# Delta-rule scan of a hybrid encoder layer: heads exchanged in four of the eight chunks, and the order of the work around them changed

## The reference, cut to what matters

```python
def step(state, inp):                     # per head: state is 64 x 64
    r_t, w_t, k_t, v_t, kk_t, a_t = inp
    s_kk = einsum('bhvk,bhk->bhv', state, kk_t)
    new = (state * w_t[:, :, None, :] - s_kk[..., None] * (kk_t * a_t)[:, :, None, :]
           + v_t[..., None] * k_t[:, :, None, :])
    read = state if reverse else new
    return new, einsum('bhvk,bhk->bhv', read, r_t)
```

## Time and profile before

| what | value |
|---|---|
| three runs | 1971.67, 1964.76 and 1939.02 us, median 1964.76 |
| the profiled execution | 1955.42 us, its span 1953.7 us |
| mean granted TensorE clock | 0.956 of full |
| PE busy, weight loads busy | 1723.0 us (88%), 1267.9 us (65%) |
| DVE, ACT, POOL busy | 1358.9 us (70%), 811.6 us (42%), 491.2 us (25%) |
| HBM traffic | 218 GB/s over the span |

### The profile page before, as it was taken

One profiled execution on the slowest core, in us unless ns is written; L12 is line 12 of the kernel. 1 busy time (PEld: TensorE's weight loads), 2 busy tenths in 40 slices (PEclk: granted clock), 3 DMA queues, 4 the chain that ended last, 5 costly groups with the idle time before them and its releaser, 6 DMA issues. The chain is left out here.

```text
span 1953.7 us, 42217 instructions
## 1 busy us (share of the span) xinstructions
PE 1723.0 (88%) x15366; PEld 1267.9 (65%) x15366; DVE 1358.9 (70%) x2513; ACT 811.6 (42%) x1327; POOL 491.2 (25%) x432
## 2 busy tenths in 40 slices
PE   3999999998688889888797699999888999999875
PEld 2787766876577778777645376666666667666532
DVE  4699996663567676765546578877766788888707
ACT  1222223441445455443300155655555566656501
POOL 2000000141644554451113013211111223332114
PEclk9899999999899999999997899999999999999988
DMA  8635853433323313222061389989888899999844
GB/s 274 193 99 173 271 171 99 130 113 98 79 44 63 66 44 72 44 61 60 3 242 54 143 314 339 371 337 345 304 304 301 314 347 345 343 351 346 326 200 199
DMA packets 259760, 389.97 MB, mean 200 GB/s; under 512 B 121923, under 2 KB 195841, under 8 KB 232240
## 3 DMA queue, kind: packets, MB, share of 16 engines
q1 hardware_dynamic: 239392, 354.28, 52.5%
q0 software_dynamic: 19872, 33.60, 4.9%
q10 hardware_dynamic: 367, 0.22, 0.1%
HBM read 368.33 MB, written 58.49 MB: 218 GB/s over the span
## 5 line engine op out<-in xcount | busy, mean ns | idle before, releaser
L2369 DVE TENSOR_TENSOR moe_w_lo<-moe_raw,moe_w_hi 128x1024 fp32r<-128x1024 f32 x272 | 315.1, 1220 | 42.8 <-ACT moe_w_hi L2295 42.6
L2295 ACT ACTIVATE moe_w_hi<-moe_raw 128x1024 fp32r<-128x1024 f32 x272 | 265.4, 1047 | 116.0 <-DMA moe_raw<-in_exp_up 115.6
L2249 PE MATMUL moe_pY<-moe_wd,moe_hT 128*128 128x512 f32 x544 | 248.1, 599 | 0.5 <-ACT moe_hT L2310 0.5
L2239 PE MATMUL moe_pH<-moe_w_hi,moe_x_hi 128*128 128x512 f32 x544 | 219.7, 404 | 12.0 <-issue 7.5
L2173 POOL DMA_INDIRECT moe_xg<-scratch_u2d,moe_idx x70 | 89.1, 1272 | 555.9 <-issue 240.4
L572 PE MATMUL proj_bank<-u_hi,w_hi 128*128 128x512 f32 x536 | 213.7, 399 | 8.4 <-PEq L74 6.8
L2239 PE MATMUL moe_pH<-moe_w_lo,moe_x_hi 128*128 128x512 f32 x544 | 214.3, 394 | 0.0
L2239 PE MATMUL moe_pH<-moe_w_hi,moe_x_lo 128*128 128x512 f32 x544 | 214.1, 394 | 0.0
L572 PE MATMUL proj_bank<-u_hi,w_lo 128*128 128x512 f32 x536 | 210.0, 392 | 0.0
L572 PE MATMUL proj_bank<-u_lo,w_hi 128*128 128x512 f32 x536 | 209.6, 391 | 0.0
L2249 PEld LDWEIGHTS moe_pY<-moe_wd,moe_hT 128*128 128x128 f32 x544 | 100.0, 194 | 100.3 <-issue 99.5
(11 more groups left out here) (414 smaller groups left out, 3139.9 us busy)
## 6 DMA issues: line engine op xcount, KB each, us to landing
moe_raw<-in_exp_gate SPq DMA_DIRECT2D x69, 1024.0 KB
moe_raw<-in_exp_up SPq DMA_DIRECT2D x69, 1024.0 KB
moe_wd<-in_exp_down SPq DMA_DIRECT2D x68, 1024.0 KB
w<-in_w_in SPq DMA_DIRECT2D x59, 512.0 KB, 7.0
pre<-in_ada_w SPq DMA_DIRECT2D x10, 2048.0 KB, 20.5
last_yb<-scratch_ybuf SPq DMA_DIRECT2D x4, 2560.0 KB, 25.5
scratch_rkv<-proj_st SPq DMA_DIRECT2D x24, 256.0 KB, 2.0
last_yb<-scratch_ybuf SPq DMA_DIRECT2D x4, 1536.0 KB, 19.8
```

What stands on the lines that cost most here:

```text
L2239: ins = nc.tensor.matmul(pH[:], a[:, k], w[p][:, k].rearrange("p w f -> p (w f)"), start=(k == 0 and n == 0), stop=(k == KC - 1 and n == 2))
L2249: ins = nc.tensor.matmul(pY[h][:], hT[:, f], wd[q][:, f, h * 512:(h + 1) * 512], start=(f == 0), stop=(f == 1))
L2295: nc.scalar.activation(w_hi[p][:, ks].rearrange("p k w f -> p w k f"), raw[p][:, :, ks], ACT.Copy) \
L2369: nc.vector.tensor_tensor(w_lo[p][:, ks].rearrange("p k w f -> p w k f"), raw[p][:, :, ks], w_hi[p][:, ks].rearrange("p k w f -> p w k f") ...
```

## The change

- **Exchanged heads.** In chunks 4 to 7 (c // NU is 1) what lies in time order has its heads exchanged: `to_time` writes head h to the other half's partitions, `to_channels` reads from the other half and writes back to the head's own. GB, GK and the four turns issue chunk u of the lower half and chunk u + 4 of the upper half alternately, into two banks; PR does it for banks 0 and 2, then 1 and 3. AC, MV, U, V and T4 stay with `by_head`, the inverse's blocks too.
- **Value products.** The output part of `base` becomes `values_read`. For the upper chunks all are issued after PR, for the lower ones with the state as before. Two semaphores come with it: `s_based` before a state's first product, `y_based` before the first lower chunk's output.
- **Order.** ZW, ZA are made for J+4 in place B5. GB moves from E (after PR) to a new place P (between AC and PR). TQ, TK, TB stand in one place each with both halves. ACT's `exps` stands ahead of C5.
- **DVE.** `scan(J + 3)` moves to the start of the job. The stages of `invert` stand as 0 between the reads of U4 and V4, 1 after those of V4, 2 between U5 and V5, 3 after V5 (before: 0 between U5 and V5, then 1 to 3 in a row). The reciprocals of the deviation and the first merge move to the end of the odd job and the start of the next. Three small instructions of stage 0 become subtractions of two tensors, with a tensor of zeros.

```diff
+FILL = {0: {"S0": (("TV", 0), ("TV", 1)), "C4": (("Z", 1), ("SS", 0)),
+            "B4": (("Z", 2), ("TQ", 0), ("TQ", 1)), "A4": (("Z", 3), ("TK", 0), ("TK", 1)), "C5": (("Z", 4), ("TB", 0), ("TB", 1)),
+            "B5": (("Z", 5), ("MV", 0), ("Z", 6), ("MV", 1), ("ZW", 0), ("ZA", 0), ("Z", 7), ("BO", 0), ("GK", 0), ("GK", 1),
                    ("MEAN", 0)),
+            "P": (("GB", 0), ("GB", 1))},
+        1: {"S0": (), "C4": (("Z", 1), ("VAR", 0)),
+            "B4": (("Z", 2), ("TQ", 0), ("TQ", 1)), "A4": (("Z", 3), ("TK", 0), ("TK", 1)), "C5": (("Z", 4), ("TB", 0), ("TB", 1)),
+            "B5": (("Z", 5), ("MV", 0), ("Z", 6), ("MV", 1), ("ZW", 0), ("ZA", 0), ("Z", 7), ("G", 0), ("GK", 0), ("GK", 1)),
+            "P": (("GB", 0), ("GB", 1))}}
...
-    of = {"Z": J - 1, "GB": J + 3, "GK": J + 1, "ZW": J + 3, "ZA": J + 3, "BO": p, "G": p, "SS": p + 2, "MEAN": p - 1,
+    of = {"Z": J - 1, "GB": J + 3, "GK": J + 1, "ZW": J + 4, "ZA": J + 4, "BO": p, "G": p, "SS": p + 2, "MEAN": p - 1,
...
-            self.take([("PR", J, k) for k in range(4)])
-            self.take(fills(J, "E"))
+            self.take(fills(J, "P"))
+            self.take([("PR", J, k) for k in (0, 2, 1, 3)])
...
+            def to_time(c, out, lhsT, rhs):
+                for h in range(2):
+                    ins = mm(out[HEADS[h ^ (c // NU)]], lhsT[HEADS[h]], rhs[HEADS[h]])
+                return ins
+
+            def to_channels(c, out, lhsT, rhs, start=True, stop=True):
+                for h in range(2):
+                    src = HEADS[h ^ (c // NU)]
+                    ins = mm(out[HEADS[h]], lhsT[src], rhs[src], start, stop)
+                return ins
...
+                o = [begin((name, q, X)) for X in range(2)]
                 for u in range(NU):
+                    for X in range(2):
+                        c = NU * X + u
+                        ins = to_time(c, o[X][:, u * P:(u + 1) * P], KB[n][:, c, 1 if name == "GB" else 0], flat(QR[n][:, c]))
+                        if u == NU - 1:
+                            end(ins, (name, q, X))
...
+            def values_read(J, c):
...
                 y = ybank[:, c * C:(c + 1) * C]
-                by_head(y, Vtm[p % 2][:, c], MKs[d][:, c, 1], True, False)
-                by_head(y, AC[:, c, 1], RB[:, c, 1], False, n == 0)
+                to_channels(c, y, Vtm[p % 2][:, c], MKs[d][:, c, 1], c == NU, False)
+                return to_channels(c, y, AC[:, c, 1], RB[:, c, 1], False, False)
...
+                    pe.wait_ge(S["s_based"], 6 * J + n)
                     by_head(sbank[n % 2][:, 0:C], RP[:, c, 1], Sb[:, n % 2], False, True).then_inc(S["s_full"], 1)
...
+                fill(J, "P")
                 if J > 0:
                     pe.wait_ge(S["s_ready"], 7 * J)
...
+                for ks in ((0, 2), (1, 3)):
+                    for k in ks:
+                        wait_read(pe, ("AC", J, k))
+                    o = [begin(("PR", J, k)) for k in ks]
+                    for m in range(2):
+                        for i, k in enumerate(ks):
+                            c = range(NCH)[pair_of(J, k)][m]
+                            ins = to_channels(c, o[i][:, m * P:(m + 1) * P], AC[:, c, 0], flat(RB[:, c, 1:3]))
...
+                for c in range(NU, NCH):
+                    ins = values_read(J, c)
+                ins.then_inc(S["y_based"], 1)
                 base(J, 0)
                 base(J, 1)
-                fill(J, "E")
+                pe.wait_ge(S["y_based"], J + 1)
+                for c in order(d)[:2]:
+                    if c < NU:
+                        values_read(J, c)
...
-                fill(J, "C5")
                 if J + 3 < JOBS:
                     exps(J + 3)
+                fill(J, "C5")
...
-                ch(nc.vector.tensor_scalar(at(X, 2, (SUB, 2)), at(A, 2, (SUB, 2)), -1.0, None, ALU.mult))
-                ch(nc.vector.scalar_tensor_tensor(at(X, 3, (SUB, 2)), at(A, 3, (SUB, 2)), -1.0, two, ALU.mult, ALU.subtract))
+                ch(nc.vector.tensor_tensor(at(X, 2, (SUB, 2), (1, 2)), free_dims(zeros[:], 0, (1, 4), (1, 2), (1, 2)), at(A, 2, (SUB, 2), (1, 2)), ALU.subtract))
+                ch(nc.vector.tensor_tensor(at(X, 3, (SUB, 2)), at(X, 3, (SUB, 2)), two, ALU.subtract))
...
-                    ch(nc.vector.tensor_scalar(flat_x[:, 1::2 * SUB + 2], flat_a[:, 1::2 * SUB + 2], -1.0, None, ALU.mult))
+                    v.wait_ge(S["zeroed"], 1)
+                    ch(nc.vector.tensor_tensor(flat_x[:, 1::2 * SUB + 2], zeros[:, 0:SUB // 2], flat_a[:, 1::2 * SUB + 2], ALU.subtract))
...
                 fill(J, "S0")
+                if J + 3 < JOBS:
+                    scan(J + 3)
+                if merging:
+                    inverse_deviation(p - 2, 2)
+                    inverse_deviation(p - 2, 3)
+                    merge(p - 2, 0)
...
-                    if j == 5 and ahead:
-                        invert(p + 1, 0)
+                    if ahead:
+                        invert(p + 1, 0 if j == 4 else 2)
...
-                    if j == 5 and ahead:
-                        invert(p + 1, 1)
-                        invert(p + 1, 2)
-                        invert(p + 1, 3)
+                    if ahead:
+                        invert(p + 1, 1 if j == 4 else 3)
```

More of the change, by code:

```diff
@@ L1369, in state @@
                     base(J, n + 1)
+                    if order(J % 2)[n + 1] < NU:
+                        values_read(J, order(J % 2)[n + 1])
             def fill(J, at):
@@ L1374, in fill @@
                         low_rank(key[1])
+                    elif key[0] in CROSSED:
+                        if key[2] == 0:
+                            (gram if key[0] in ("GB", "GK") else turn)(key[0], key[1])
                     elif key[0] != "ZA":
-                        {"Z": state, "TV": turn, "TQ": turn, "TK": turn, "TB": turn, "MV": values, "GB": gram, "GK": gram,
-                         "SS": norm_kk, "BO": bonus, "G": gate, "MEAN": mean,
+                        {"Z": state, "MV": values, "SS": norm_kk, "BO": bonus, "G": gate, "MEAN": mean,
                          "VAR": variance}[key[0]](key)
             for q in range(2):
-                for X in range(2):
-                    gram(("GB", q, X))
+                gram("GB", q)
             low_rank(2)
             norm_kk(("SS", 1, 0))
-            for X in range(2):
-                gram(("GK", 0, X))
+            gram("GK", 0)
+            low_rank(3)
             for J in range(JOBS):
@@ L1754, in _ @@
                             merge(p - 2, 3)
[L1755 to L1757 removed]
                         fill(J, "A4")
[L1759 to L1762 removed]
+                fill(J, "P")
+                for k in (0, 2, 1, 3):
                     o = wait_full(v, ("PR", J, k))
@@ L1769, in _ @@
                 if ended:
-                    merge(p - 1, 0)
-                fill(J, "E")
-            for n in range(1, 4):
+                    inverse_deviation(p - 1, 0)
+                    inverse_deviation(p - 1, 1)
+            inverse_deviation(PAIRS - 2, 2)
+            inverse_deviation(PAIRS - 2, 3)
+            for n in range(4):
                 merge(PAIRS - 2, n)
```

64 lines of the change are left out of this document (24 added, 40 removed), and 5 rows, old and new, of the table FILL.

## The result

The changed kernel takes **1932.6 us** (median of 20 runs, 1913.9 to 1964.2) against 1971.3 for the kernel before in 20 runs beside it, 39 us less. The ratio is **0.9898, with a 95% interval of 0.9852 to 0.9944**: about 20 us faster (11 to 29), where 51 were forecast. The ratio compares fast runs alone, those within 1.5% of a kernel's fastest (14 of the 20 after, 7 of the 20 before), which is why it shows a smaller gain than the two medians do. 1932.6 lies just above the forecast's own range (1897 to 1930) and inside the wide one (1880 to 1946). The profiled execution has a span of 1932.3 us at a mean granted clock of 0.937.

The account below looks back on a forecast made before the run. PE's own work was taken to bound even jobs, the hole ahead of AC and the inverse's loop odd ones. Savings of 27 + 2 + 22 = 51 us from 1955.4 gave 1904, or 1914 for a median; own range 1897 to 1930.

Parts of the forecast that it names:

- what the exchange does: Turns, GB, GK and PR on PE: four quarters run together, halving 8.8 us, so 4.4 us of PE time a job.
- The rival in which quarters take turns: Exchanged passes on PE: quarters on the same rows alternate, only the order gains, 22 us, so 1943; chance 0.18.
- the one in which a weight load waits: Exchanged passes on PE: a quarter's load waits for the matmul on the same rows, up to 2055; chance 0.04.
- the new hole and its place: Odd jobs: DVE waits 2.9 us for the blocks with V4's reads behind, opening about 4 us ahead of T4.
- 3.4 saved, times 8 is 27 us: Even jobs: 24.2 us against 27.6, PE's own work less the exchange's gain, over eight jobs.
- 3.7 for six jobs, 22 us: Odd jobs: U4 at 29.3 against 33.5, taken as 3.7 for six jobs and none for job 13.
- the way to Tn is unchanged, 11.4: Loop of the inverse, from X and XT ready to the next U4: stays 11.4 us.
- what stands behind the wait: Odd jobs: V4's reads, T4, ACT's copies and U5 follow the wait for the blocks; U5 read at 12.6 us.
- job 15: Last odd job, no inverse and no GB: TQ, TK, TB and PR halve, saving 2.3 us.
- the wait in the middle eats the odd job: Rival: stage 0 behind the blocks, small steps held by POOL, PE at 1.2 GHz; odd jobs stay 33.5, 1935; chance 0.15.
- The clock: Even jobs: 1.0 us added for slower banks and a 1.2 GHz start; odd jobs: 1.0 for 1.2 GHz after the hole.
- The rule of the Trainium skill: Stage 0's small steps: two-SBUF-input DVE instructions contend with GpSimd, so the edit buys nothing; without it 1.9 us a pair.

Follow-up runs that it names:

- e2: Changed kernel with the heads not exchanged, all of its order kept: jobs 0 to 14 take 429.9 us against 417.1, ratio to before 0.9966.
- the two second profiles: The changed kernel and the kernel before, each profiled once more unaltered: jobs 0 to 14 take 415.3 and 443.7 us.
- e4: Changed kernel with stages 0 and 1 of the inverse both after the reads of V4: jobs 0 to 14 take 392.3 us, ratio to before 0.9884.
- e16: Changed kernel with only the inverse's way back to Tn cut short, stage 0 still ahead of V4's reads: jobs 0 to 14 409.0 us, ratio to before 0.9756.
- e1: Changed kernel with dummy products on PE ahead of T4 and of the wait for Tn: jobs 0 to 14 take 408.2 us, ratio to before 0.9844.
- e5: e4's kernel with dummy products on PE where it waited: jobs 0 to 14 take 394.7 us against 392.3, ratio to before 0.9839.
- e10: Changed kernel with exps back behind ACT's copies of C5: jobs 0 to 14 take 435.4 us, ratio to before 0.9972.
- e8: Changed kernel with stage 0's three small steps in their old form (times -1): jobs 0 to 14 take 412.3 us, ratio to before 0.9978.
- e9: e4's kernel with four DMA issues less between XT and Tn: jobs 0 to 14 take 393.5 us, ratio to before 0.9660.
- e7: Kernel before with only the inverse's stages spread, 0 and 1 behind the reads of V4: jobs 0 to 14 take 449.3 us, ratio to before 1.0057.

## Why the prediction was wrong

**Right: what the exchange does.** Half the time for the turns, GB and PR; 44.5 us less work on PE in 15 jobs by e2, 3.0 a job, less than the 4.4 forecast and at a lower clock. The rival in which quarters take turns, and the one in which a weight load waits, are out. One reading behind it was not what its own numbers say: ZW and ZA, which share columns, take 133 / 256 = 0.52 ns a column, two diagonal quarters 57.5 / 128 = 0.45, so sharing columns was not shown free, and that it held for these products is in part luck. The rule of Part 3 in TensorE: Matmul & The Clock Gate (the Trainium skill), that a load overlaps only matmuls on other rows, would have been that second rival; no turn in the trace shows it.

**Right: the new hole and its place.** No wait on MK, DVE 4.19 us on the blocks where 2.9 were expected, 4.16 ahead of T4 where about 4 were.

**Wrong: "3.4 saved, times 8 is 27 us".** The level was right: 24.2 forecast, 24.5 measured (196.3 / 8). What failed is the baseline. I took 27.6 from one even job for all eight; they average 26.4 (210.9 / 8), since the first one and the last two take 23.5 to 24.5. Saved: 14.6 us (19.5 between the two second profiles). One view by job of all 15 would have shown it.

**Wrong: "3.7 for six jobs, 22 us".** Measured: 3.9 over seven (8.9 between the two second profiles). Part is the baseline again (33.5 taken, 32.8 the mean of the six). The rest is the loop: 29.8 a job forecast, 31.7 measured. The forecast took three things off it, 4.3 us in all. The loop starts earlier, 1.9 us ahead of U4 and not 0.8: measured 1.7. DVE's wait of 1.6 to reach stage 0 goes: measured 1.3. And the middle, from stage 0 to XT, shrinks from 14.0 to 12.4 while "the way to Tn is unchanged, 11.4": **that step failed**. Over the first six pairs the middle went only from 13.6 to 13.2, and the way from 10.7 to 12.1; the blocks took 0.3 longer too (8.1, where 7.35 were taken). So the loop is as long as before (33.5 against 33.6), and what the odd jobs won, 1 us each, is that it starts earlier. Of the 1.4 on the way 1.1 lies in the write-out: its last piece lands 6.0 us after XT, where it was 4.9; why stays open. I had costed all of it from one pair of jobs. Job 13, for which nothing was taken, lost 2.5 us (27.9 to 30.4): its middle is 11.5 us long where it was 8.4, and its blocks land 1.5 later.

**Seen, and priced too low: what stands behind the wait.** The forecast had the reads of V4, T4, U5 and the read of U5 in a row behind the wait for the blocks and ahead of stage 2, done 12.6 into the job; in the job above they are done at 13.5. What it did not ask is whether that row had to be in the loop. e4 takes it out: the reads of V4 come ahead of the wait, the middle falls by 2.1 us to 11.0, the loop by 2.9 and the odd jobs by 20 us in all. e16, which leaves the row and shortens the way instead, takes 24 us off the odd jobs. Both are what a loop that bounds them would do.

**Wrong: job 15.** 2.3 were to be saved; from its U4 to the end of the last variance product it takes 31.5 us against 28.4. 1.2 of the 3.1 are there when the mean product starts, which waits 1.77 us for the output where it waited 0.78; the other 1.9 are the mean and variance products themselves, 2.07 us each at 1.2 GHz where they took 1.12. The four reciprocals, which lay beside PE's work, stand in a row at the job's end, ahead of the merge and the output; that they make the wait is likely, no run moves them:

```profile
940.36 3.38 DVE L1625 RECIPROCAL rwkv_rstd<-rwkv_rstd 128x128 f32<-128x128 f32 x4
...
946.62 0.68 DVE L1700 TENSOR_TENSOR rwkv_yf<-rwkv_yt,rwkv_ybank 128x512 f32<-128x512 f32 x1
```

**The sum.** 27 + 22 + 2 = 51 against 14.6 + 3.9 - 3.1 = 15.4 to the end of the scan; the remaining 6 of the 21.4 between the spans lie outside it, in work that the change does not touch and that differs as much between executions. The rival "the wait in the middle eats the odd job", at 1935 and a chance of 0.15, was nearer: 30 us of gain, and the wait did eat most of it. Its other half, small steps held by POOL, shows in some jobs and not in others: in the job above they take 0.17 us each, but in two of the seven odd jobs the first one took 1.2, and in five the copy ahead of them 0.9 to 1.3 instead of 0.37. That 1932.6 lies 2.4 from its 1935 is luck: it took 30 us off a base of 1964.8, the median of three runs, where twenty give 1971.3 and the ratio a gain of 20. The rival in which quarters take turns had 22 us, nearest to that 20, by a mechanism that is out.

**The clock** was taken, with the slower banks, as 1.0 us a job, some 15 in all. It was at 1.2 GHz for 85 us, against 31, and half of the 54 more would be 27 us if PE were the bound. Halving the slow time won 9 us net in e1 and nothing in e5, each with other changes in the loop against it. The price is not contradicted, and not shown.

**The rule of the Trainium skill** (SBUF — State Buffer, "Who interferes with whom"), by which the new form of the small steps buys nothing, agrees with the traces: beside a POOL product the new form takes 1.21 us and the old one 1.20 (e8 and the changed kernel), and jobs 0 to 14 are no longer with the old form.

Open: why the blocks land 6.6 us after the GB read in some pairs and 10.1 in others (the move of SP's loads was not tried), why the write-outs of X and XT, and with the dummies those of GB, land later than before, and why e10 is as slow as before.

## What to carry to other kernels

Where engines pass a value round a loop that is as long as the period, work taken from one of them that lies outside the loop changes who waits, not the period: here it shortened the even jobs and not the odd ones. Write the loop's legs down for every period, not for one, and shorten a leg first: moving one wait in one queue took 25 us off the jobs, halving some 200 matmul passes a job 13 to 21. And before an operation is moved "where the engine is idle", ask what keeps it idle: e9 gained 24 us in one kind of job and gave it back in the other, to work that had been put into idle time which only the old wait had made.

## What the hardware showed

- Four 64 x 64 quarters of fp32 matmuls run together when two share their rows and two their columns: 29 ns a pass of 128 columns for 57.5 with two quarters.
- A copy of 64 x 256 on DVE took 0.37 us alone, 0.38 where it began together with a POOL product, and 1.33, 1.20 and 1.37 (after, e7, e4) where it began 0.13 to 0.30 us after one and ended 0.2 us behind it. A small step of 128 x 8, 0.17 alone, took 1.20 or 1.21 in the same place, whether it reads one tensor or two (e8, after). Two small products that take 0.45 us together took 2.57 in e7 beside POOL's of 1.3 each.
- The fetch of one 64 KB block landed 4.0 us after its issue in the changed kernel and 3.2 before, with the same two loads of 256 KB issued right behind it in both.
